# Where the low parts of the weights are made, and the order of VectorE's work inside a head

## The reference, cut to what matters

```
kk = einsum("bhnik,bhnjk->bhnij", k, k)
lhs = where(strict, beta * kk * decay, 0) + eye(64)          # per chunk of 64 tokens
sol = triangular_solve(lhs, rhs, lower=True, unit_diagonal=True)
v_new = u_c - w_c @ state                                     # scan over the chunks
o_c = (q_c * exp(g_c)) @ state + attn_c @ v_new
log_a = -8 * r * softplus(-lam)                               # RG-LRU, scan over time
h_t = exp(log_a) * h_{t-1} + sqrt(-expm1(2 log_a)) * (i * xc)
```

## Time and profile before

| | us |
|---|---|
| median of 3 runs | 1655.18 (1652.72 to 1655.63) |
| the profiled execution, whole | 1654.16 |
| its span in the profile | 1651.9 |
| DVE busy in the span | 674.7 (41%) |
| POOL busy in the span | 205.4 (12%) |
| PE busy in the span | 1456.4 (88%) |

### The profile page before, as it was taken

One profiled execution on the slowest core, in us unless ns is written; L12 is line 12 of the kernel. 1 busy time (PEld: TensorE's weight loads), 2 busy tenths in 40 slices (PEclk: granted clock), 3 DMA queues, 4 the chain that ended last, 5 costly groups with the idle time before them and its releaser, 6 DMA issues.

```text
span 1651.9 us, 21189 instructions
## 1 busy us (share of the span) xinstructions
PE 1456.4 (88%) x7998; PEld 888.6 (54%) x7998; DVE 674.7 (41%) x1128; ACT 438.5 (27%) x839; POOL 205.4 (12%) x151
## 2 busy tenths in 40 slices
PE   5888989989888789698998998989989989989985
PEld 4887887888887667533433433534434334334332
DVE  5866676675776554512122121312213222222223
ACT  5434344345254234411111110111111111112112
POOL 2333133232232324000000000000000000000000
PEclk9899999999999899799999999999999999999998
DMA  7632442443435236489999999999999999999994
GB/s 203 156 87 70 117 118 76 105 105 102 105 101 164 77 102 228 180 351 429 426 429 426 428 428 428 429 428 429 428 429 428 429 428 429 427 430 428 428 427 184
DMA packets 145588, 479.97 MB, mean 291 GB/s; under 512 B 11209, under 2 KB 111762, under 8 KB 120082
## 3 DMA queue, kind: packets, MB, share of 16 engines
q1 hardware_dynamic: 145554, 479.50, 74.2%
HBM read 477.39 MB, written 2.10 MB: 290 GB/s over the span
## 4 chain that ended last, share of the span: by engine, by line
PE 52%; DMA 22%; DVE 15%; issue 5%; ACT 5%; SPq 1%; DVEq 0%; ACTq 0%
PE bank L541 51%; DMA ew<-in_expert_w_dram 21%; DVE w_parts L1251 2%; PE bank L544 1%; DVE misc L1383 1%; ACT w_parts L954 1%; DVE ew L1290 1%; DVE misc L1382 1%; DVE ye L1283 1%; DVE ye L1352 1%; ACT ew L1164 1%; DVE ye L1290 1%; ACT L984 1%; ACT fw_r L1129 0%; DMA fw<-in_norm_ffn_w_dram 0%
## 5 line engine op out<-in xcount | busy, mean ns | idle before, releaser
L541 PE MATMUL bank<-ew,hT 128*64 128x512 f32 (+1 forms) x1600 | 475.5, 597 | 44.7 <-DMA ew<-in_expert_w_dram 30.4
L541 PE MATMUL bank<-act_parts,w_parts 128*128 128x256 f32 x2304 | 336.7, 299 | 19.5 <-DVE w_parts L1251 14.8
L541 PEld LDWEIGHTS bank<-ew,hT 128*64 128x64 f32 (+1 forms) x1600 | 158.3, 140 | 348.1 <-issue 344.2
L541 PEld LDWEIGHTS bank<-act_parts,w_parts 128*128 128x128 f32 x2304 | 302.0, 200 | 32.7 <-DVE w_parts L1251 16.6
L541 PE MATMUL bank<-ew 128*64 128x512 f32 (+1 forms) x1056 | 237.2, 593 | 8.4 <-DVE ew L1652 6.8
L541 PE MATMUL bank<-mixT,hT 128*64 128x512 f32 x512 | 228.6, 600 | 0.0
L1650 DVE SCALAR_TENSOR_TENSOR ew<-ew,bank 128x256 f32<-128x256 f32 x32 | 13.5, 421 | 465.8 <-ACT ew L1166 465.8
L1716 POOL TENSOR_TENSOR w_parts<-fw,w_parts 128x768 fp32r<-128x768 f32 x64 | 138.8, 2174 | 325.7 <-ACT w_parts L954 325.5
L541 PEld LDWEIGHTS bank<-ew 128*64 128x64 f32 (+1 forms) x1056 | 76.5, 139 | 148.0 <-issue 134.7
L1181 ACT ACTIVATE ye_r<-bank 64x512 fp32r<-64x512 f32 x128 | 68.7, 585 | 281.4 <-PE bank L541 280.6
L1164 ACT ACTIVATE ew<-bank,gs 128x512 f32<-128x512 f32 x32 | 22.0, 687 | 435.6 <-PE bank L541 435.6
(11 more groups left out here) (237 smaller groups left out, 1253.4 us busy)
## 6 DMA issues: line engine op xcount, KB each, us to landing
ew<-in_expert_w_dram SPq DMA_DIRECT2D x160, 2048.0 KB, 16.5
mixT<-in_expert_w_dram SPq DMA_DIRECT2D x32, 2048.0 KB, 19.0
fw<-in_w_in_dram SPq DMA_DIRECT2D x48, 1024.0 KB, 5.8
fw<-in_w_out_dram SPq DMA_DIRECT2D x16, 1024.0 KB, 5.0
mixT<-in_x_dram SPq DMA_DIRECT2D x1, 2048.0 KB, 7.5
fw<-in_x_dram SPq DMA_DIRECT2D x1, 2048.0 KB, 10.0
out_dram<-fw SPq DMA_DIRECT2D x2, 1024.0 KB, 3.9
fw<-in_norm_final_w_dram SPq DMA_DIRECT2D x1, 1024.0 KB, 20.2
```

The source lines that it names most:

```text
L541: return nc.tensor.matmul(o, l, r, start=start, stop=stop, skip_group_check=True)
```

## The change

Three edits. GpSimd makes no low parts any more: each `rest` on VectorE covers all 2048 columns, and the waits for `s_restP` go. In a head, VectorE makes `aa` before `qg` (L1364), then the inverse step at once, and then the low part of block two (`between("levels", 0)`), ahead of convolution zero (`pre(0)`). The RG-LRU part is spread: its first two products stand behind level one, its scan and last product behind level three.

```diff
             def slot_free(g):
                 sp.wait_ge(s_restD, g - RING + 1)
-                sp.wait_ge(s_restP, g - RING + 1)
             def wait_piece(g):
                 pe.wait_ge(s_restD, g + 1)
-                pe.wait_ge(s_restP, g + 1)
...
                 dve.wait_ge(s_high, g * 2 + 2)
-                V.tensor_tensor(wparts[:, slot, 1, 0:SPLIT], raw[:, slot, 0:SPLIT], wparts[:, slot, 0, 0:SPLIT],
+                V.tensor_tensor(wparts[:, slot, 1, :], raw[:, slot, :], wparts[:, slot, 0, :],
                                 ALU.subtract).then_inc(s_restD, 1)
...
                 dve.wait_ge(s_qkT, h + 1)
-                V.scalar_tensor_tensor(qg..., QSCALE, egb..., ALU.mult, ALU.mult).then_inc(s_qg, 1)
                 dve.wait_ge(s_kk, h + 1)
                 dve.wait_ge(s_dec, h * 2 + 2)
                 V.tensor_tensor(aa..., bank[5][:, :], dec..., ALU.mult).then_inc(s_aa, 1)
-                pre(0)
+                V.scalar_tensor_tensor(qg..., QSCALE, egb..., ALU.mult, ALU.mult).then_inc(s_qg, 1)
...
                                 ALU.subtract).then_inc(s_T, 1)
                 between("start", 0)
-
-                link(V.scalar_tensor_tensor(lru[:, 1], lru[:, 1], 1.0, xc, ALU.add, ALU.mult))
-                dve.wait_ge(s_mu, h + 1)
-                link(V.scalar_tensor_tensor(lru[:, 2], lru[:, 1], 0.5, lru[:, 4], ALU.mult, ALU.mult))
-                link(V.tensor_tensor_scan(lru[:, 0], lru[:, 3], lru[:, 2], 0.0, ALU.mult, ALU.add))
-                V.tensor_tensor(lru[:, 1], lru[:, 0], gg, ALU.mult).then_inc(s_y, 1)
                 between("levels", 0)
+                pre(0)
                 for lv in range(1, LEVELS):
                     dve.wait_ge(s_U, h * (LEVELS - 1) + lv)
                     V.tensor_tensor(tt..., tt..., bank[2][:, :], ALU.subtract).then_inc(s_T, 1)
+                    if lv == 1:
+                        link(V.scalar_tensor_tensor(lru[:, 1], lru[:, 1], 1.0, xc, ALU.add, ALU.mult))
+                        dve.wait_ge(s_mu, h + 1)
+                        link(V.scalar_tensor_tensor(lru[:, 2], lru[:, 1], 0.5, lru[:, 4], ALU.mult, ALU.mult))
                     if lv == 2:
                         pre(1)
+                    if lv == 3:
+                        link(V.tensor_tensor_scan(lru[:, 0], lru[:, 3], lru[:, 2], 0.0, ALU.mult, ALU.add))
+                        V.tensor_tensor(lru[:, 1], lru[:, 0], gg, ALU.mult).then_inc(s_y, 1)
                     if lv == 4:
                         pre(2)
...
-            def rest(g, slot):
-                pool.wait_ge(s_high, g * 2 + 2)
-                G.tensor_tensor(wparts[:, slot, 1, SPLIT:], raw[:, slot, SPLIT:], wparts[:, slot, 0, SPLIT:],
-                                ALU.subtract).then_inc(s_restP, 1)
```

More of the change, by code:

```diff
@@ L48 @@
 RING = 3
-SPLIT = 1280
 COMB = (6, 7, 0, 1)
@@ L311, in build @@
         s_restD = sem("s_restD")
-        s_restP = sem("s_restP")
         s_hH = sem("s_hH")
@@ L1363, in heads @@
                 dve.wait_ge(s_qkT, h + 1)
-                V.scalar_tensor_tensor(qg.rearrange("p (t i) -> p t i", t=NT),
-                                       bank[4][:, :].rearrange("p (t b i) -> p t b i", t=NT, b=2)[:, :, 0, :], QSCALE,
-                                       egb.rearrange("p (t i) -> p t i", t=NT), ALU.mult, ALU.mult).then_inc(s_qg, 1)
                 dve.wait_ge(s_kk, h + 1)
@@ L1370, in heads @@
                                 dec.rearrange("p t b i -> p (t b i)"), ALU.mult).then_inc(s_aa, 1)
-                pre(0)
+                V.scalar_tensor_tensor(qg.rearrange("p (t i) -> p t i", t=NT),
+                                       bank[4][:, :].rearrange("p (t b i) -> p t b i", t=NT, b=2)[:, :, 0, :], QSCALE,
+                                       egb.rearrange("p (t i) -> p t i", t=NT), ALU.mult, ALU.mult).then_inc(s_qg, 1)
                 idb = ident.rearrange("p (a i) -> p a i", a=1).broadcast_to([P, NT, P])
@@ L1711, in heads @@
                     G.tensor_tensor(atm[:, lv], aa[:, :, 1, :], m.broadcast_to([P, NT, P]), ALU.mult).then_inc(s_atm, 1)
-            def rest(g, slot):
-                pool.wait_ge(s_high, g * 2 + 2)
-                G.tensor_tensor(wparts[:, slot, 1, SPLIT:], raw[:, slot, SPLIT:], wparts[:, slot, 0, SPLIT:],
-                                ALU.subtract).then_inc(s_restP, 1)
             pool.wait_ge(s_cst, 16)
             G.tensor_copy(tri_one[:, :], cst[:, C_TRI:C_TRI + 2 * P]).then_inc(s_tri, 1)
-            for g in range(8):
-                rest(g, g % RING)
             decays(0)
@@ L1725, in _ @@
                 heads(i - 1)
-                for b in range(6):
-                    rest(i * 6 + b + 2, (b + 2) % RING)
                 decays(i)
             heads(NH - 1)
-            for m in range(2, 8):
-                rest(NH * 6 + m, m % RING)
             for n, lo, hi in ((3, 4, 7), (4, 12, 15)):
@@ L1735, in _ @@
                     .then_inc(s_mixLP, 1)
-            for m in range(8, 16):
-                rest(NH * 6 + m, m % RING)
 _INS = ["x", "norm_mix_w", "w_in", "gdn_conv_w", "gdn_a_log", "gdn_dt_bias", "gdn_norm_w", "rg_conv_w", "rg_conv_b",
```

## The result

The changed kernel takes 1625.56 us, the median of four runs (1621.33 to 1628.63), the kernel before 1654.75 beside it (four runs, 1652.72 to 1655.63). The ratio is 0.9828, with a 95% interval of 0.9813 to 0.9842. The profiled execution is the slowest of the four, 1628.63 with a span of 1626.8, 25.1 less than the span before.

The account below looks back on a forecast made before the run. In a head VectorE sets the pace up to block two, then TensorE. Terms 3.5 + 3.2 + 1.2 + 3.0 = 10.9 us off 1654.16 give 1643.3; the median lies 1.0 higher, so 1644, range 1630 to 1656 (main case 1636 to 1651).

Parts of the forecast that it names:

- ahead of the first `aa`: Prologue: TensorE's 2.92 us wait nearly goes and its 48 matmuls may run faster; 3.5 us less, bounds 1 and 5.
- first head: No reciprocal in its level three, so a level-four stall of 0.6 instead of 2.3; 3.2 us less in all.
- heads one to six: Six heads, each with the product w 0.2 us earlier: 1.2 us less.
- last head and end: Level two's wait of 4.25 us shrinks as the scan group leaves; 3.0 us less, nothing for the tail.
- the sign of being wrong that I had named: The forecast counts as wrong if, among other signs, heads take over 65.5 us or under 62.5.
- I take 1.5 stretches at 1.3, 1.9 us: w is 0.2 earlier: In a head, low-clock stretches behind the two new gaps take back 1.9 of the 2.1 us gained up to w.
- up to 2.9 more if the clock holds: Prologue: 48 matmuls behind TensorE's gap, 8.58 us before, could gain up to 2.9 us at full clock.
- The clock holds: Rival: all gain is kept in heads, first head, last head and prologue; 27 us less, 1628, chance 0.17.
- The level-four stall wins: Rival: the scan's 2.19 us is mostly its own work, stall 3.8 instead of 2.3; slower, 1661, chance 0.10.
- Only relocation: Rival: the prologue's wait passes to ScalarE or the load and heads lose 0.8 us; no change, 1655, chance 0.13.
- The exclusion for whole instructions: Two-input VectorE and SBUF-reading GpSimd instructions exclude each other; convolution zero would end near 356.5 instead of 355.5.

Follow-up runs that it names:

- e6_keep_warm: The changed kernel plus matmuls whose result nobody reads, 18 ahead of level two and 14 ahead of level five: 1623.25 us.
- e9_first_eight: The kernel before, with VectorE making the whole low part of the first eight pieces only: 1646.34 us against 1654.3.
- e2_order_only: The changed kernel's order with the low parts still shared with GpSimd as in the kernel before: 1654.54 us, ratio 0.9997 to the kernel before.
- e7_fit_shared: The order of e4 with the low parts shared with GpSimd again (768 columns): 1629.67 us, ratio 0.9847 to the kernel before.
- e1_split_only: The kernel before, in its old order, with VectorE making all 2048 columns of each low part: 1621.5 us against 1653.79.
- e3: The changed kernel, with GpSimd also subtracting its old 768 columns in the heads into unread memory, TensorE and the loads waiting for it: 1679.03 us.
- e5_pool_unwaited: The changed kernel, with GpSimd also subtracting 768 columns of unused memory per block in the heads, neither TensorE nor VectorE waiting for it: 1682.85 us.
- e8: The changed kernel with convolution zero moved from ahead of level one's subtraction to behind it: 1629.01 us.
- e4: The changed kernel with VectorE's work spread so each level's share fits TensorE's 3.5 us, the rest moved behind the levels: 1588.69 us.

## Why the prediction was wrong in size

I set the terms of the sum beside the two profiles of the changed kernel, measured from one `aa` to the same one of before. The second profile (1625.11) lies next to the median.

| term | predicted | first profile | second profile |
|---|---|---|---|
| ahead of the first `aa` (89.78 before) | 3.5 | 4.9 | 7.6 |
| first head (63.90) | 3.2 | 4.5 | 3.2 |
| heads one to six (391.63) | 1.2 | 12.1 | 15.0 |
| last head and end | 3.0 | 3.6 | 2.9 |
| sum | 10.9 | 25.1 | 28.7 |

**What held.** The mechanism in a head came out nearly row by row. No wait ahead of level one and block two (right); 2.51 ahead of level two (2.9); almost none ahead of level three (0.5); 2.04 ahead of level five (2.3); the scan at 0.69 (0.68); the low part at 2.29 to 2.38 (2.38); level one's subtraction done at `aa` + 9.2 (9.6). From `aa` to w it takes 26.05 us in head four against 28.96 in the earlier trace rows, 2.9 less, where I had 2.1 with the clock full throughout; in head one of the changed kernel, with two low stretches, w comes at 173.08, 28.86 behind `aa`: 0.1 less, where I had 0.2. A head at the old clock takes 64.2 and 64.0, where I had 64.2. The heads at full clock, with 61.4, are the sign of being wrong that I had named (under 62.5).

**What failed** in the heads, 1.2 us forecast where 12.1 and 15.0 came, is one step: "I take 1.5 stretches at 1.3, 1.9 us: w is 0.2 earlier", argued from "the new gaps, 2.9 and 2.3, are as long as the present ones, which mostly bring one each". The gaps were as long as I said. They brought two low stretches each in heads one and two of the first profile; in the second, two in head one and one in the first head. In the others up to head five there were none. TensorE's busy time over heads one to six was 348.1 us before and 338.8 after, by the windows of all six: 9.4 of the 12.1 us are its matmuls at a higher clock, and 2.6 a shorter idle time, 1.8 of it in head one. With the two gaps filled (`e6_keep_warm`) no head up to five had a low stretch, which fits, but in one execution only. Why a gap of 2.5 us is followed by a low stretch in head one and not in head three, with the same instructions ahead, no run here settles. Their distance is a rival to their length that I left untested: before, the waits of 2.67 and 1.80 us ended 6.4 us apart (352.42 and 358.78), now those of 2.51 and 2.04 end 13.1 apart (343.14 and 356.25). My second error in that step was to carry over a count from a profile in which it was already seen to vary: head two of before had one stretch less than its neighbours.

The prologue was mis-sized in part for the same reason. Its wait fell by 2.42 as computed (2.4), but of "up to 2.9 more if the clock holds" I took 1.1, and the 48 matmuls gained 2.6. Two terms were missing from the sum: the first block begins 1.0 us earlier (1.5 in the second profile), since TensorE had waited for GpSimd's part there, and the block ahead of the first head takes 6.02 us for its 48 matmuls in the second profile where it took 7.51. `e9_first_eight` puts the part at 8.0, outside my bounds of 1 to 5. The first profile shows only 4.9 of it, since a low stretch fell on the matmuls of the block behind (8.53 us for 48; 6.02 in the second).

**The rivals.** "The clock holds", 1628 with a chance of 0.17, came nearest, 2.4 us off, and part of that is luck. Its terms were 14 for the heads, 4.5, 3.7 and 4.5; measured in the second profile are 15.0, 3.2, 2.9 and 7.6. It took every head to keep the clock at 2.1 to 2.5 us each; in fact heads three to five gained 3.1 each and head one 1.4. "The level-four stall wins" fell with the scan at 0.69. "Only relocation" (1655) fell for the changed kernel. It is what `e2_order_only` shows (1654.5), though for a reason I had not given: with GpSimd's low parts in place, this order only chose which VectorE instructions were long beside them. It is no rule for every order, as `e7_fit_shared` gained 25.

**What I credited wrongly.** In the sum the reordering carried the heads' gain (inverse step first, 3.2 us at level two); the freed GpSimd was counted in the prologue and as a scan of 0.68 us. The runs reverse it: the split alone gives 31 to 32 us, the order alone 0. In `e1_split_only` the wait ahead of level one stays and the one ahead of block two shrinks to 1.16 or, behind a low stretch, to nothing; in the changed kernel both go, but 2.51 comes ahead of level two, and level five has 2.04 instead of 0.98. At full clock a head takes 61.3 with the one and 61.4 with the other. I had seen these two gaps coming and still booked the order as a gain of its own. Nor does the split pay by shorter waits in a head at full clock: TensorE's idle time there is 5.4 to 5.6 us in both kernels with the split and was 5.5 to 5.7 before. What those heads gained is the clock. That GpSimd's low parts cost this is shown (`e1`, `e3`, `e5`); by which step they keep the clock lower is open.

**The rule weighed.** The exclusion for whole instructions (the Trainium skill, page "SBUF — State Buffer", section "Who interferes with whom") I had priced as a convolution zero that ends a us later than by the rows; its subtraction ended at `aa` + 9.2, 0.5 earlier than the rows gave, so as I priced it the rule missed. As the page states it, the traces agree better with it than with my reading of a fixed surcharge. The added time depends on what stands beside it: 0.35 us per convolution instruction beside masks, 1.1 beside low parts in `e5_pool_unwaited` (4.71 less 1.52, over three), 1.5 for L1382 and for the scan. L1382 and the scan, and the convolutions of `e2_order_only` and `e5_pool_unwaited`, end within 0.6 us behind the end of a GpSimd instruction.

## What to carry to other kernels

An instruction that takes 1.5 us longer than its like elsewhere may be waiting inside its own duration, and moving it may only move the wait: look at what the other engine does in the same microseconds, and take that work away (32 us here, where this reordering gave 0). Then sum an engine's work between the fixed ties of a loop against the pace of the engine that should set it; an order that leaves one sum too large moves the wait to another level (`e8`), one in which all of them fit removes it (37 us in `e4`). And where gaps are followed by a lower clock in some rounds of a loop and not in others, forecast both cases as a range: 2.8 us per head lay on it in the changed kernel, and only 0.2 in `e1`, where the low stretch fell on a wait.

## What the runs showed of the chip

- GpSimd's subtractions of 768 columns, 42 of them, unread and not waited for by TensorE or VectorE, cost 57 us of the whole, with 88.4 us of their own duration (`e5_pool_unwaited`). Left to GpSimd, 768 columns took 1.83 us at best, where VectorE takes 0.8 more for them (2.29 less 1.49).
- The interference is mutual: a mask takes 0.73 us where it is quickest and 2.77 beside VectorE's low part of 2048 columns, both in the head of the changed kernel shown above.
- The same heads, with the same instructions and the same idle time, take 61.4 or 64.1 us by the granted clock (a mean of 1.00 or 0.95). Which of the two it is differs from execution to execution, and the four runs of the changed kernel spread over 7.3 us with clocks of 0.968 to 0.975.
